# Two transformer blocks on one core: attention by pairs of heads in halves of the array, values projected by tokens

## The reference, cut to what matters

```python
h = rmsnorm(x, g_mix_pre)
p = h @ w_in                                   # 256 x 5920: all queries, keys, values, gates
# NSA, per head: o = g0*cmp + g1*slc + g2*win  (one key/value pair per group of 4 heads)
#   cmp: 15 compressed keys, from gelu(blocks of 32 keys @ w1) @ w2
# moba, fox (bias = cumulated log forget gates), dilated: one softmax(q k^T * scale + bias) v per head
s = q @ k.T * scale + bias;  o = softmax(where(mask, s, NEG)) @ v        # 256 queries, 256 keys
x = x + rmsnorm(concat(o_a, o_b, o_c, o_d) @ w_out, g_mix_post)
x = x + rmsnorm(square(relu(rmsnorm(x, g) @ w_up)) @ w_down, g_mlp_post)
...
m = silu(c) @ w_ada + b_ada                    # 2048 x 12288, for the second block: shifts, scales, gates
```

## Time and profile before

| | |
|---|---|
| median of 3 runs | 2799.28 us (2798.76 to 2803.87) |
| the profiled execution, its own time | 2800.81 us |
| its span, first to last instruction | 2799.0 us |
| mean granted TensorE clock | 0.987 |
| busy: PE, DVE, ACT, POOL | 98%, 66%, 47%, 9% |
| bytes moved, mean rate | 572.93 MB, 205 GB/s |

### The profile page before, as it was taken

One profiled execution on the slowest core, in us unless ns is written; L12 is line 12 of the kernel. 1 busy time (PEld: TensorE's weight loads), 2 busy tenths in 40 slices (PEclk: granted clock), 3 DMA queues, 4 the chain that ended last, 5 costly groups with the idle time before them and its releaser, 6 DMA issues.

```text
span 2799.0 us, 43810 instructions
## 1 busy us (share of the span) xinstructions
PE 2735.7 (98%) x18584; PEld 2500.9 (89%) x18584; DVE 1850.0 (66%) x2300; ACT 1324.2 (47%) x1745; POOL 265.1 (9%) x265
## 2 busy tenths in 40 slices
PE   8999999899999999999999999999999999999998
PEld 8988887679899898898899989999889899898996
DVE  5466666679999977778766675666554555545555
ACT  4244444344444344346776435566554444344443
POOL 1112222000000000001011031111000000000010
PEclk9899999999999999999999999999999999999999
DMA  9644644737777778778656544444555655655553
GB/s 316 235 160 168 203 163 143 258 135 270 270 282 260 290 266 294 273 285 308 194 156 192 181 152 141 151 136 151 178 163 171 195 191 186 195 182 195 189 188 120
DMA packets 287042, 572.93 MB, mean 205 GB/s; under 512 B 9798, under 2 KB 28525, under 8 KB 286528
## 3 DMA queue, kind: packets, MB, share of 16 engines
q1 hardware_dynamic: 280736, 548.69, 57.8%
q0 software_dynamic: 6112, 21.45, 2.6%
HBM read 566.30 MB, written 3.27 MB: 203 GB/s over the span
## 4 chain that ended last, share of the span: by engine, by line
PE 89%; DVE 4%; ACT 3%; DMA 2%; issue 1%; POOL 1%; SPq 0%; DVEq 0%; ACTq 0%
PE p_gemm L1882 49%; PE p_gemm L1903 30%; DMA ada_w<-in_w_ada 1%; DVE w_lo L1141 1%; ACT w_hi L670 1%; PE p_b L1973 1%; PE p_ada L1923 1%; PE p_b L2018 1%; PE p_b L2017 1%; PE p_b L2029 1%; PE p_b L2044 1%; PE p_b L2270 0%; PE p_b L2208 0%; PE p_b L2104 0%; PE p_b L2217 0%
## 5 line engine op out<-in xcount | busy, mean ns | idle before, releaser
L1141 DVE TENSOR_TENSOR w_lo<-w_raw,w_hi 128x1024 fp32r<-128x1024 f32 (+1 forms) x864 | 1071.9, 1244 | 764.8 <-ACT w_hi L670 763.6
L670 ACT ACTIVATE w_hi<-w_raw 128x1024 fp32r<-128x1024 f32 (+1 forms) x864 | 896.8, 1041 | 1270.2 <-PE p_gemm L1882 784.9
L1882 PE MATMUL p_gemm<-h_hi,w_hi 128*128 128x256 f32 x3184 | 914.5, 287 | 9.1 <-DVE w_lo L1141 4.8
L1882 PE MATMUL p_gemm<-h_lo,w_hi 128*128 128x256 f32 x3184 | 898.7, 282 | 0.0
L1882 PE MATMUL p_gemm<-h_hi,w_lo 128*128 128x256 f32 x3184 | 898.2, 282 | 0.0
L1882 PEld LDWEIGHTS p_gemm<-h_hi,w_hi 128*128 128x128 f32 x3184 | 604.5, 190 | 26.5 <-issue 15.2
L1882 PEld LDWEIGHTS p_gemm<-h_lo,w_hi 128*128 128x128 f32 x3184 | 604.7, 190 | 0.3
L1882 PEld LDWEIGHTS p_gemm<-h_hi,w_lo 128*128 128x128 f32 x3184 | 604.3, 190 | 0.0
L1903 PE MATMUL p_gemm<-w_hi,a_hi 128*128 128x512 f32 x1024 | 400.2, 391 | 0.0
L1903 PE MATMUL p_gemm<-w_hi,a_lo 128*128 128x512 f32 x1024 | 398.7, 389 | 0.0
L1903 PE MATMUL p_gemm<-w_lo,a_hi 128*128 128x512 f32 x1024 | 398.5, 389 | 0.0
(11 more groups left out here) (347 smaller groups left out, 2415.8 us busy)
## 6 DMA issues: line engine op xcount, KB each, us to landing
w_raw<-in_w_mlp SPq DMA_DIRECT2D x128, 1024.0 KB, 5.2
w_raw<-in_w_in SPq DMA_DIRECT2D x108, 1024.0 KB, 5.4
ada_w<-in_w_ada SPq DMA_DIRECT2D x96, 1024.0 KB, 5.2
w_raw<-in_w_up SPq DMA_DIRECT2D x64, 1024.0 KB, 8.2
w_raw<-in_w_down SPq DMA_DIRECT2D x64, 1024.0 KB, 8.6
w_raw<-in_w_out SPq DMA_DIRECT2D x32, 1024.0 KB, 5.5
w_raw<-in_w_in SPq DMA_DIRECT2D x36, 768.0 KB, 4.7
cmp_w<-in_phi_w POOLq DMA_DIRECT2D x2, 2048.0 KB, 15.9
```

The lines of the kernel that those rows point to most:

```text
L670: act.activation(WH[:, s % 4, :, 0:n], RAW[:, s // 2, 2 * (s % 2):2 * (s % 2) + 2, 0:n], ACT.Copy)\
L1141: dve.tensor_tensor(WL[:, s % 4, :, 0:n], RAW[:, s // 2, 2 * (s % 2):2 * (s % 2) + 2, 0:n], WH[:, s % 4, :, 0:n].bitcast(F32), ALU.subtrac ...
L1882: ins = pe.matmul(dst, w[:, s % 4, kk, cols], x[:, k, :], start=k == 0 and m % 2 == 0 and i == 0, stop=k == KC - 1 and i == 2, skip_group_ ...
```

## The change

1. **Pairs.** 24 pairs take the place of 48 units. The two heads of a pair lie in partitions 0 to 63 and 64 to 127 of a chunk; their scores are issued alternately, one with rows 0 to 63 of the array into one PSUM bank, one with rows 64 to 127 into another. The values' products alternate between columns 0 to 63 and 64 to 127, and the first block of keys is multiplied with the probabilities of both blocks of queries at once (256 columns). Elementwise work is done for both heads in one instruction where it can be, on `[128, 2, 384]`. Pairs start every 3 slots; transposes come 4 slots later, the product with the values 5.
2. **Values by tokens.** Chunks are reordered (`CHUNKS`), so that value chunks fill blocks 2, 5 and 8 and half of 11. Those go by tokens in `project_half`; `turn_values` is gone.
3. **Compression turned round.** The 30 columns are stationary, 256 weight columns move, and both `w1` are loaded ahead into buffers of their own. The gelu works on 30x512 and its result is transposed back (`compress_turn`).
4. **The adaptive vector later.** Its steps, tiles and totals leave blocks 0 to 15 and go to blocks 16 to 47, 56 to 61 and 70 to 79.
5. **Smaller moves.** The filter's steps in `w_out` come 1 to 3 slots earlier, the filter's constants and the bias tables are loaded earlier.

```diff
+CHUNKS = (["qa0", "qa1", "qa2", "qa3"], ["kc", "vc", "ks", "misc"], ["vs", "vw", "vd0", "vd1"], ["kw", "qd0", "kd0", "qd1"],
+          ["kd1", "qd2", "kd2"], ["vd2", "vd3", "vf0", "vf1"], ["qd3", "kd3", "qf0", "kf0"], ["qf1", "kf1", "qf2", "kf2"],
+          ["vf2", "vf3", "vm0", "vm1"], ["qf3", "kf3", "qm0", "km0"], ["qm1", "km1", "qm2", "km2"], ["qm3", "km3", "vm2", "vm3"])
+V_BLOCKS, V_HALF = (2, 5, 8), 11
-B_ADA, ADA_BLOCKS = 0, 48
+ADA_BLOCKS = [*range(16, 48), *range(56, 62), *range(70, 80)]
-F_MM, F_SIN = (7, 10), (8, 11)
+F_MM, F_SIN = (6, 8), (7, 9)
...
+        PAIRS = [(k, r) for k in ("slc", "win", "cmp", "dil", "fox", "moba") for r in range(4)]
-        D_INV, D_T, D_PV = 1, 2, 3
+        D_INV, D_T, D_PV = 1, 4, 5
+        START = [24] + [27 + 3 * u for u in range(1, NU - 1)] + [WIN_SLOTS + 1]
-        S_Z, S_CMM = (19, 23), (20, 24)
+        S_Z, S_CMM, S_GELU = (18, 20), (19, 21), 23
...
             def compress(kv):
-                for m in range(2):
-                    for j in range(16):
-                        ins = pe.matmul(ps[:, 30 * m:30 * m + 30], W1C[:, j, P * m:P * m + P], CZ[:, j, :, :],
-                                        start=j == 0, stop=j == 15)
+                for j in range(16):
+                    ins = pe.matmul(ps[0:30, 0:T], CZ[:, j, :, :].rearrange("p g c -> p (g c)"), W1C[kv][:, j, :],
+                                    start=j == 0, stop=j == 15)
...
             def scores(u):
-                pe.matmul(ps[:, 0:n0], q[:, 0:P], k[:, 0:n0], start=True, stop=True)
-                pe.matmul(ps[:, P:P + n1], q[:, P:T], k[:, 0:n1], start=True, stop=True).then_inc(S("scores_ready"), 1)
+                for z, keys, col in parts:
+                    for g in range(2):
+                        rows = slice(HD * g, HD * g + HD)
+                        ins = pe.matmul(ps[g][:, col:col + keys.shape[-1]], q[rows, P * z:P * z + P], keys[rows, :],
+                                        start=True, stop=True)
...
             def weighted_values(u):
-                    pe.matmul(out[0], v[0], PTS[:, 0:P], start=True, stop=True)
-                    pe.matmul(out[1], v[0], PTS[:, P:2 * P], start=True, stop=False)
-                    pe.matmul(out[1], v[1], PTS[:, 2 * P:3 * P], start=False, stop=True).then_inc(S("pv_ready"), 1)
+                    for blk, queries, probs in ((0, slice(0, T), slice(0, T)), (1, slice(P, T), slice(T, 3 * P))):
+                        for g in range(2):
+                            ins = pe.matmul(ps[HD * g:HD * g + HD, queries], PJ[:, CH[vc], P * blk + HD * g:P * blk + HD * g + HD],
+                                            PTS[:, g, probs], start=blk == 0, stop=blk == 1, skip_group_check=True)
...
+            def compress_turn():
+                pe.wait_ge(S("gelu_ready"), 1)
+                ps = bank(CMP_BANKS[0], "cmp_read", 3)
+                for kv in range(2):
+                    for m in range(2):
+                        col = 60 * kv + 30 * m
+                        ins = pe.transpose(ps[:, col:col + 30], GT[:, 2, kv, P * m:P * m + P], IDN[0:30, 0:30])
+                ins.then_inc(S("cmp_turned"), 1)
```

More of the change, by code:

```diff
@@ L360, in unit_bank, with pair @@
-        def unit_bank(u):
-            return u % 3
+        S_Z, S_CMM, S_GELU = (18, 20), (19, 21), 23
+        S_MISC, MISC_BANK = 19, 1
+        CMP_BANKS = (2, 3)
+        FOX_SLOT = [START[U_DIL + 1 + r] + D_PV for r in range(4)]
+        OUT_AT = {"dil": CH["qa0"], "fox": CH["vs"], "moba": CH["kw"]}
+        def pair(u):
+            kind, r = PAIRS[u]
+            if u < U_DIL:
+                return kind, r, f"qa{r}", {"slc": "ks", "win": "kw"}.get(kind), {"slc": "vs", "win": "vw"}.get(kind)
+            return kind, r, f"q{kind[0]}{r}", f"k{kind[0]}{r}", f"v{kind[0]}{r}"
@@ new lines, in bias, with attended, pair_banks, soft @@
+        def bias(u):
+            r = PAIRS[u][1]
+            return BX[:, r:r + 5:4, :] if u < U_DIL else BX[:, 2 * r:2 * r + 2, :]
+        def attended(u):
+            kind, r = PAIRS[u]
+            return OA[:, r, :] if u < U_DIL else PJ[:, OUT_AT[kind] + r, :]
+        def widths(u):
+            return (NCMP0, NCMP) if PAIRS[u][0] == "cmp" else (P, T)
+        def pair_banks(u):
+            return PBS[:, 2 * (u % 2):2 * (u % 2) + 2, :]
+        def soft(u, what):
+            at0 = 12 * (u % 2) + 4 * ("max", "sum", "inv").index(what)
+            return TINY[:, at0:at0 + 4]
@@ L406, in mix_src @@
         def mix_src(m):
-            return mixer_out(MIX_CHUNKS[m]) if m < 3 else mixer_out(CH_B)[:, 2 * (m - 3):2 * (m - 3) + 2, :]
+            if m == 0:
+                return OA[:, :, :]
+            first = OUT_AT[("dil", "fox", "moba", "moba")[m - 1]] + (2 if m == 4 else 0)
+            return PJ[:, first:first + (4 if m < 3 else 2), :]
         block = ctx.enter_context(nc.Block())
@@ L463, in _ @@
             sp.dma_start(IDN[:, :], a["ident"]).then_inc(S("ident_loaded"), 16)
-            blocks(B_WIN, 12, a["w_in"])
+            for b in range(B_WOUT):
+                for j in range(4):
+                    weight_tile(b, j, rows(a["w_in"], j * 4 * P, P * CH_AT[b], P * block_chunks(b)))
             blocks(B_WOUT, 4, a["w_out"])
@@ L1174, in ada_step @@
                 ins.then_inc(S("ada_summed"), 1)
-            def plain_block(b):
-                for s in range(UPB):
-                    slot(b, None, s)
             def sum_parts(n, cols):
@@ L1799, in _ @@
                 m = b - B_WOUT2
-                plain_block(b)
+                for s in range(UPB):
+                    slot(b, None, s)
+                    ada_step(b, s)
+                    if m == 1 and s == 0:
+                        modulation(2)
                 dve.wait_ge(S("unit_used"), count(b + 1, None, UPB))
@@ L2007, in scores @@
             def scores(u):
-                kind, qc, kc, _, p0, _ = unit(u)
-                ps = bank(unit_bank(u), "logits_ready", u + 1)
-                pe.wait_ge(*gemm_read(max(qc, kc or 0) // 4))
-                q, k = PJ[p0:p0 + HD, qc, :], None if kind == "cmp" else PJ[p0:p0 + HD, kc, :]
+                kind, r, qc, kc, _ = pair(u)
+                ps = [bank(2 * (u % 2) + g, "logits_ready", u + 1) for g in range(2)]
+                pe.wait_ge(*gemm_read(max(CH_BLOCK[qc], CH_BLOCK[kc] if kc else 0)))
@@ L2346 @@
     misc = np.concatenate([part[7], np.zeros((D, 8), f), part[14], np.zeros((D, 88), f)], 1)
-    by_pair = [part[f + j][:, i * P:i * P + P] for f in (15, 11, 8) for i in range(4) for j in range(3)]
-    w_in = np.concatenate([part[0][:, pairs], *part[1:7], misc, *by_pair], 1)
+    named = {"kc": part[1], "vc": part[2], "ks": part[3], "vs": part[4], "kw": part[5], "vw": part[6], "misc": misc}
+    for i in range(4):
+        named[f"qa{i}"] = part[0][:, pairs[P * i:P * i + P]]
+        for mixer, f0 in (("d", 15), ("f", 11), ("m", 8)):
+            for j, side in enumerate("qkv"):
+                named[f"{side}{mixer}{i}"] = part[f0 + j][:, i * P:i * P + P]
+    w_in = np.concatenate([named[c] for c in CH], 1)
     wo = x["w_out"][0]
```

487 lines of the change are left out of this document (262 added, 225 removed).

## The result

The changed kernel takes 2735.84 us (median of 4 runs, 2726.88 to 2739.07) against 2799.02 us (4 runs): a ratio of 0.9765 with a 95% interval of 0.9738 to 0.9792, faster by 63 us. The forecast was 2714 us, its range 2694 to 2742. So the direction and the range held, and the forecast promised 22 us more than came. The profiled execution has a span of 2731.0 us against 2799.0, where the sum had said 2713.5.

The account below looks back on a forecast made before the run. PE's own work was taken to bound the attention stage, with waits and low clock a second loss. Terms of -48 -3.6 -1.9 -20 -9 +1 +1 -5 -1 +1 sum to -85.5 us, giving 2714 us, range 2694 to 2742.

Parts of the forecast that it names:

- a low clock in the compressions: Part of the rival of larger new waits: compression at the lower clock costs up to 13.8 us more; rival's chance 0.15.
- One of its own signs of being wrong: The prediction is wrong if PE waits for splits behind 1513 us.
- Pairs, -48: Attention units: 48 at 2.3 us (110.4) become 24 pairs at 2.6 us (62.4), saving 48 us.
- 2.3 each: Attention stage before the change: 101 us left for about 44 of the 48 units, 2.3 us each.
- The rival on column halves: Pairs' value products: column halves don't overlap, price 24 x 0.6 = 15 us, giving 2729 us; chance 0.2.
- Entries cheaper for pairs, and no wait between scores and transposes: Pairs: three entries of 0.1 us per pair instead of per head; no wait expected with 3.5 slots for elementwise work.
- V turns, -3.6: Value chunks: fourteen times two transposes go, 0.3 us a chunk; twelve chunks outside the first stretch save 3.6 us.
- By tokens, -1.9: Projection blocks 5 and 8 done by tokens gain 0.9 us each, 1.9 us saved.
- Up to the small products, at 123.1: Compression's small products start at 123.1 us instead of 141.9, with a new gelu wait of 4.1; saves 20 us (14 to 25).
- Adaptive vector out of `w_out`, -9: Stage of `w_out`: less waiting on weights and the sine, some 3 us less low clock; saves 9 us (6 to 12).
- POOL -5, transition +1: Wait on POOL before moba goes, -5 us with the clock; uncovered rounding of mixer's output between projection and `w_out`, +1.
- DVE in the later blocks, +1 (0 to 6): Later blocks: eight more DVE steps a block, just enough room in block 60, less loaded in 70 to 79; costs 1 us.

Follow-up runs that it names:

- run 3: The changed kernel with both heads' score products on the same 64 rows and value products into the same 64 columns: 2756.25 us.
- runs 1 and 2: The changed kernel with a pair's score products (first run) or value products (second) issued head after head instead of alternating: 2735.27 and 2734.83 us.
- run 9: The changed kernel with the second compression's 2 MB of weights asked for later, behind the copies of the compressed keys: 2729.93 us.
- run 10: The changed kernel with the first part of the mixer's output copied and rounded two to four slots before the projection's end: 2727.33 us.
- Run 5: The changed kernel with the adaptive vector's steps in blocks 70 to 79 made on 32 of their 512 columns: 2722.61 us.
- the second measurement of the same kernel: The changed kernel itself, unchanged, measured again beside later variants: 2732.93 us (5 runs, 2727.05 to 2736.28).

## Why the prediction came out 17.5 us short of the span

The prediction's stated range held, but the narrower one to which it gave half its chance, 2705 to 2724 us, did not. That the wide range held is partly luck: it was wide for rivals that did not come (column halves, a low clock in the compressions), and what fell short was something else. One of its own signs of being wrong did show: behind 1513 us PE waits 5.3 us for a split, where before it waited 2.6 at the same place:

```profile
PE p_gemm L1903 <- DVE w_lo L1141: 2.6, 1, 2.6
```

Its sum says 92.9 us until block 16 and 7.4 given back there. These are the 85.5, with the 1 for DVE's later steps, and with 6.4 for the adaptive vector's sums that move to the later part. The prediction gave a sum no price of its own. In the kernel before seven of its eight sums lie ahead of block 16, and each costs PE's stream 0.92 us. Measured are 85.4 and 17.4: 7.5 and 10.0 short.

- **Pairs, -48: right in kind, 3 too large.** Adding PE's start-to-start times on the attention's lines up to block 16 gives 90.7 us before, 4.3 of them the wait on POOL, and 50.7 after, 2.0 of them new waits on turned probabilities: 86.4 against 48.7. Going in and out costs the stream 18.5 us more in 112 visits, and 11.5 in 71. Together -44.7: the units cost 104.9 us and not 110.4, the pairs 60.2 and not 62.4. The step that failed is "2.3 each": it divides what was left of a stage by 44 heads. The eight heads on compressed keys cost less, 0.54 us for scores (the timeline of before, first and last row) where others take 0.85, and 0.58 for values where others take 0.80, so that pairing them saves about 2 us less:

```profile
232.22 0.38 PE L2017 MATMUL p_b<-cmp_kT,proj 64*128 64x7 f32 x2
...
232.76 0.39 PE L1882 MATMUL p_gemm<-h_hi,w_hi 128*128 128x256 f32 x1
```

- **The rival on column halves** fell by the values' 0.80 us and by run 3: they take 0.80 us in two halves and 1.41 in one. Lying in different halves decides it, not the order of issue (runs 1 and 2). The rule of the Trainium skill ("TensorE: Matmul & The Clock Gate", What overlaps and what doesn't), by which column halves would wait for their weight loads, doesn't hold for these rows: the load for the second head starts 5 ns behind the first head's product.
- **Entries cheaper for pairs, and no wait between scores and transposes**: so it is. But there are three waits of 2.0 us in all one step later, between transposes and values, on ACT's copy of the turned probabilities: two in early pairs, one in a pair on compressed keys. Entries are fewer, not cheaper: 0.16 us a visit in both kernels.
- **V turns, -3.6**: the lines of the turns took 5.8 us in all, 5.6 of them here; better by 2. **By tokens, -1.9**: about 0.5. The term took the pace of the last MLP, 21.8 us a block; in the projection a product of 512 columns starts each 0.234 us, so that 96 take 22.5.
- **Up to the small products, at 123.1**: they start at 128.70. Compressions and the gelu's wait are as forecast. The step that failed is block 1, "without a wait, 22.7": it takes 27.7, and though it starts 1.9 us early, block 2 begins 3.1 late. Block 2 adds 1.8, about the cost of the low clock from 71.2 to 74.6 us. The wait of 4.1 us behind an adaptive tile was replaced by waits of 1.7 and 2.9 on split weights, whose tile is 28.31 us under way. The prediction looked for the wait in DVE and SP and forgot that the change also adds a transfer of 2 MB there. By run 9, with that transfer later, 4.1 of these 4.6 us go.
- **Adaptive vector out of `w_out`, -9**: the stage is 15.2 us shorter. 1.7 of it are sums, and 2.4 are products of units and pairs, counted above. About 11 are left, better by 2: PE's waits fall by 6.9, and the clock is at 1.2 GHz for 6.8 us instead of 17.4.
- **POOL -5, transition +1**: the wait on POOL is gone, as forecast. The transition is as forecast, +1: the wait of 2.6 us became 3.6, and the low clock behind it fell from 5.3 us (454.4 to 459.7) to 3.4. What the prediction missed is that this wait stood there already, so that it could be taken away. In run 10 it is gone, and block 16 starts 4.4 us earlier.
- **The rest up to block 16.** These terms account for some 6 of the 7.5 us; the rest was not traced.
- **DVE in the later blocks, +1 (0 to 6)**: the largest miss. Block 60 was judged rightly: DVE is busy for 22.35 of 25.60 us (0.87, a little less than the 90% forecast) and PE waits for nothing there. But "in blocks 70 to 79 it is less loaded" went by DVE's share over the block, 0.54 to 0.61. In 70 to 72 PE waits for chains that pass through DVE, and DVE has the added steps to make between their links: blocks 70 to 75 are 9.8 us longer, 1.8 of it two sums, and 8.0 PE's waits (5.5 more) and the clock. Run 5 gives back 9.0. Another 1.5 us or so is a stretch of low clock at 1327 us that the second measurement of the same kernel doesn't have. The last 1.3 us of the 17.4 were not traced.

## What to carry to other kernels

In this kernel two half-size products in different row or column halves cost what one costs; count how many visits and which sizes they replace unit by unit, never by dividing a stage. When work is moved to an engine because its share of busy time is low, look for a chain through that engine that the bound engine waits for in that stretch: there part of the added work is paid (31.2 us more on DVE in blocks 70 to 75 cost 8 to 9), while block 60 at 0.87 busy paid nothing. Before calling a wait new, look for it in the kernel before. And when a change removes a wait by taking a transfer away, look at what else the change loads in the same microseconds.

## What was not expected of the hardware

The products of the two halves need not be issued alternately: with four score products of one head issued before four of the other, the pair still takes 0.86 us, and in the trace the second head's first product starts 13 to 14 ns behind the first head's first (6 to 7 ns when issued alternately). And a busy PE can still be at the low clock: with PE busy for 51.23 of 51.40 us in the old form of the compression the mean granted clock was 0.74, and with 38.90 of 39.70 in the new form 0.96. Within one compression of the old form the products start every 0.112 us at 2.4 GHz and every 0.213 at 1.2 GHz, with no wait between them where the clock falls.
